# The gate table by one f32r matmul of 256 columns a token, split into a high and a low half

## What is computed

```python
qh = (xb @ w_query).reshape(tb, PEER_HEADS, 2, PEER_HALF)
scores = jnp.einsum('thpc,hpnc->thpn', qh, keys32)
val, idx = lax.top_k(scores, PEER_TOPK)
...
ids = jnp.take_along_axis(cand_id, pos, axis=-1).reshape(tb, PEER_HEADS * PEER_TOPK)
gate = jax.nn.softmax(top_s, axis=-1).reshape(tb, PEER_HEADS * PEER_TOPK)
```

## Time and profile before

| | |
|---|---|
| median of 3 runs | 3603.85 us (3603.44 to 3604.87) |
| the profiled execution | 3609.25 us, its span 3607.6 us |
| PE matmul busy | 3499.1 us, 97% |
| VectorE (DVE) busy | 1775.3 us, 49% |
| ScalarE (ACT) busy | 1278.5 us, 35% |
| GpSimd (POOL) busy | 509.7 us, 14% |

### The profile page before, as it was taken

The page is one execution under the profiler, slowest core; times in us unless marked ns, Lnnn a source line. Parts: engine busy times, 40 slices in busy tenths (PEclk is TensorE's granted clock), DMA queues, the critical chain, the costliest instruction groups (busy, mean ns, idle before and its releaser), DMA issues. The chain is left out here.

```text
span 3607.6 us, 52575 instructions
## 1 busy us (share of the span) xinstructions
PE 3499.1 (97%) x19436; PEld 2987.0 (83%) x19436; DVE 1775.3 (49%) x3405; ACT 1278.5 (35%) x1843; POOL 509.7 (14%) x434
## 2 busy tenths in 40 slices
PE   8998999999999999999999999998999999889999
PEld 8956787788888878888888799998889789768887
DVE  7344599566665224444444533335445456553333
ACT  4244222466665232222222332223223333333232
POOL 0100115433332001111111010010100000121011
PEclk9999999999999999999999999999999989989999
DMA  4200224355555546666666322222222100122232
GB/s 148 76 18 18 88 94 140 123 175 174 176 183 185 189 147 192 190 191 192 194 192 196 119 87 95 87 94 70 94 83 77 57 1 1 36 71 101 91 98 72
DMA packets 115447, 416.05 MB, mean 115 GB/s; under 512 B 14192, under 2 KB 14320, under 8 KB 113008
## 3 DMA queue, kind: packets, MB, share of 16 engines
q1 hardware_dynamic: 75632, 279.93, 23.6%
q0 software_dynamic: 18944, 67.12, 6.3%
q10 hardware_dynamic: 20736, 67.12, 4.9%
HBM read 344.91 MB, written 69.21 MB: 115 GB/s over the span
## 5 line engine op out<-in xcount | busy, mean ns | idle before, releaser
L444 DVE TENSOR_TENSOR w_lo<-ring,w_hi 128x1024 fp32r<-128x1024 f32 x224 | 275.5, 1230 | 695.6 <-ACT w_hi L440 695.5
L183 DVE TENSOR_TENSOR w_lo<-ring,w_hi 128x1024 fp32r<-128x1024 f32 (+2 forms) x157 | 205.9, 1312 | 571.5 <-ACT w_hi L177 571.5
L440 ACT ACTIVATE w_hi<-ring 128x1024 fp32r<-128x1024 f32 x255 | 270.1, 1059 | 504.4 <-PE ps L490 487.3
L460 PE MATMUL ps<-hn_hi,w_hi 128*128 128x512 f32 x1024 | 408.3, 399 | 3.0 <-POOL w_lo L444 1.4
L460 PE MATMUL ps<-hn_lo,w_hi 128*128 128x512 f32 x1024 | 404.8, 395 | 0.0
L460 PE MATMUL ps<-hn_hi,w_lo 128*128 128x512 f32 x1024 | 403.1, 394 | 0.0
L490 PE MATMUL ps<-units_hi,w_hi 128*128 128x512 f32 x1024 | 398.4, 389 | 2.7 <-DVE units_lo L801 2.7
L490 PE MATMUL ps<-units_hi,w_lo 128*128 128x512 f32 x1024 | 398.4, 389 | 0.0
L490 PE MATMUL ps<-units_lo,w_hi 128*128 128x512 f32 x1024 | 398.3, 389 | 0.0
L177 ACT ACTIVATE w_hi<-ring 128x1024 fp32r<-128x1024 f32 (+2 forms) x170 | 190.2, 1119 | 470.1 <-PE ps L241 379.7
L241 PE MATMUL ps<-f_hn_hi,w_hi 128*128 128x264 f32 (+1 forms) x1056 | 283.6, 323 | 19.8 <-DVE f_hn_lo L861 19.1
(11 more groups left out here) (434 smaller groups left out, 6719.2 us busy)
## 6 DMA issues: line engine op xcount, KB each, us to landing
ring<-in_w_uv SPq DMA_DIRECT2D x256, 512.0 KB, 3.4
ring<-in_f_up SPq DMA_DIRECT2D x88, 512.0 KB, 3.3
expert_units<-scratch ACTq DMA_DIRECT2D x128, 256.0 KB, 2.6
gate_table<-peer ACTq DMA_DIRECT2D x16, 2048.0 KB, 7.2
peer<-gate_table POOLq DMA_DIRECT2D x32, 1024.0 KB, 7.7
peer<-expert_units POOLq DMA_DIRECT2D x128, 256.0 KB, 3.7
ring<-in_w_in SPq DMA_DIRECT2D x29, 512.0 KB, 3.3
ring<-in_w_late SPq DMA_DIRECT2D x25, 512.0 KB, 3.3
```

The source lines that it names most:

```text
L183: self.nc.vector.tensor_tensor(self.l[:, self.slot(k), 0:self.cols], e.ring[:, self.ring(k), 0:self.cols], self.h[:, self.slot(k), 0:self. ...
L440: A_(uh[:, slot(n)], e.ring[:, ring(n), 0:D], ACT.Copy).then_inc(e.hi_done, 1)
L444: ops.tensor_tensor(ul[:, slot(n)], e.ring[:, ring(n), 0:D], uh[:, slot(n)].bitcast(F32), ALU.subtract).then_inc(e.lo_done, 1)
L460: mm = M(e.ps[:, n % 2, :], u[:, slot(n), ch * P:(ch + 1) * P], x[part][:, ch, META:L], start=(ch == 0 and j == 0), stop=(ch == DC - 1 and ...
```

## The change

A token's outer product becomes one f32r matmul: the stationary side is the column one-hot in f32r, the moving side 256 columns wide, with the row one-hot times the high part of the gate and the row one-hot times the low part side by side. The gate is split once for all tokens into `tb.gates` (high by ScalarE, low by VectorE). A batch now fills two PSUM banks, with two batches in turn instead of four. ScalarE copies the high half to an SBUF buffer (`high`), and VectorE adds the low half to it from PSUM and writes the table (`evac`, now VectorE's). VectorE makes no columns any more; ScalarE makes those of all odd batches. `hots` writes into 4 places in place of 8. VectorE's queue for each tile is now `hots`, `lo`, `hots`, `evac`, `evac`.

```diff
         def outers(it, m):
...
-            if r % 4 == 1:
-                pe.wait_ge(hot_act, it * 4 + (m // 4 + 1))
+            pe.wait_ge((hot_pool, hot_act)[m % 2], it * 8 + (m // 2 + 1))
             pe.wait_ge(stored, it * 16 + (m + 1))
             for t in range(GT):
-                mm = M(e.ps[:, 4 + m % 4, t * P:(t + 1) * P], tb.cols[:, r, t], tb.rows[:, r, t])
+                mm = M(both(m)[:, t].rearrange("p x i -> p (x i)"), tb.cols[:, m % GR, t],
+                       tb.rows[:, m % 4, t].rearrange("p x i -> p (x i)"))
...
-        def evac(it, m):
-
-            blk = m // BK
-            if m % BK == 0:
-                act.wait_ge(saved[blk], it * 16 + 16)
+        def high(it, m):
+
             act.wait_ge(outer, it * 16 + (m + GR + 1))
...
+            A_(tb.high[m % 2], both(m)[:, :, 0], ACT.Copy).then_inc(copied, 1)
...
-                A_(y[:, n * P:(n + 1) * P], e.ps[:, 4 + n, j * P:(j + 1) * P], ACT.Copy)
...
+            A_(tb.gates[:, n * P:(n + 1) * P, 0], e.ps[:, 4 + n, 2 * P:3 * P], ACT.Copy).then_inc(spread, 1)
...
-        columns(0, 1)
-        columns(0, 5)
+        for m in (1, 3, 5):
+            columns(0, m)
...
         def table_step(it, n, more):
             hi(act, it, 8, AHEAD + n + 1)
+            if more:
+                columns(it, 2 * n + 7)
             gelu(it, 8, AHEAD + n)
             spill(it, 8, AHEAD + n - 1)
-            evac(it, 2 * n)
-            evac(it, 2 * n + 1)
-            if n % 2 == 0 and more:
-                columns(it, 2 * n + 1 + GR)
+            high(it, 2 * n)
+            high(it, 2 * n + 1)
...
         def hots(it, m):
...
-            dve.wait_ge(outer, it * 16 + (m + 1))
+            dve.wait_ge(outer, it * 16 + (m + GR - 4 + 1))
...
-                oh = V.tensor_scalar(tb.rows[:, r, t], c["iota"], e.rowT[:, bass.ds(col, 1)],
-                                     e.gateT[:, bass.ds(col, 1)], ALU.is_equal, ALU.mult)
-                if r % 4 == 3:
-                    oh = V.tensor_scalar(tb.cols[:, r, t], c["iota"], e.colT[:, bass.ds(col, 1)], None,
-                                         ALU.is_equal)
+                oh = V.scalar_tensor_tensor(out=tb.rows[:, m % 4, t],
+                                            in0=c["iota"].unsqueeze(1).broadcast_to([P, 2, P]),
+                                            scalar=e.rowT[:, bass.ds(col, 1)],
+                                            in1=parts.unsqueeze(2).broadcast_to([P, 2, P]),
+                                            op0=ALU.is_equal, op1=ALU.mult)
...
+        def evac(it, m):
...
+            dve.wait_ge(copied, it * 16 + (m + 1))
+            t0 = (m % BK) * GT
+            V.tensor_tensor(tb.table[:, blk].rearrange("p i t -> p t i")[:, t0:t0 + GT, :], tb.high[m % 2],
+                            both(m)[:, :, 1], ALU.add).then_inc(stored, 1)
+
+        def table_step(it, n, more):
+            if more:
+                hots(it, 2 * n + 2)
+            lo(dve, V, it, 8, AHEAD + n + 1)
+            if more:
+                hots(it, 2 * n + 3)
+            evac(it, 2 * n)
+            evac(it, 2 * n + 1)
...
+        V.tensor_tensor(tb.gates[:, :, 1], e.gateT, tb.gates[:, :, 0].bitcast(F32), ALU.subtract).then_inc(parted, 1)
+        dve.wait_ge(parted, 1)
+        hots(0, 0)
+        hots(0, 1)
```

More of the change, by code:

```diff
@@ L418, in phase_peer @@
     hot, hot_pool, hot_act = e.sem("hot"), e.sem("hot_pool"), e.sem("hot_act")
+    parted, copied = e.sem("gate_parts"), e.sem("high_copied")
     pool_offset, act_offset = e.sem("pool_offset"), e.sem("act_offset")
@@ L445, in lo, with both @@
                           ALU.subtract).then_inc(e.lo_done, 1)
+    def both(m):
+        at = (4 + 2 * (m % 2)) * WIDE
+        return e.psf[:, at:at + 2 * WIDE].rearrange("p (t x i) -> p t x i", t=GT, x=2)
     def sp_program(sp):
@@ L482, in mix @@
                 if first and o == 4:
-                    pe.wait_ge(stored, batches + 4)
+                    pe.wait_ge(stored, batches + 2)
                 if first and o == 0:
@@ L528, in act_program @@
             act.sem_inc(saved[s], 16)
-        act.sem_inc(stored, 4)
         def gelu(it, step, n):
@@ L548, in columns @@
             off.then_inc(act_offset, 1)
-            act.wait_ge(act_offset, it * 4 + (m // 4 + 1))
-            A_(tb.cols[:, m % GR], tb.cols[:, m % GR], ACT.Relu, bias=e.one, scale=-1.0).then_inc(hot_act, 1)
-        def evac(it, m):
-            blk = m // BK
-            if m % BK == 0:
-                act.wait_ge(saved[blk], it * 16 + 16)
+            act.wait_ge(act_offset, it * 8 + (m // 2 + 1))
+            A_(tb.cols[:, m % GR], tb.cols[:, m % GR].bitcast(F32), ACT.Relu, bias=e.one,
+               scale=-1.0).then_inc(hot_act, 1)
+        def high(it, m):
             act.wait_ge(outer, it * 16 + (m + GR + 1))
-            t0 = (m % BK) * GT
-            A_(tb.table[:, blk].rearrange("p i t -> p t i")[:, t0:t0 + GT, :],
-               e.ps[:, 4 + m % 4, :].rearrange("p (t i) -> p t i", t=GT), ACT.Copy).then_inc(stored, 1)
+            A_(tb.high[m % 2], both(m)[:, :, 0], ACT.Copy).then_inc(copied, 1)
         def save(it, blk):
-            act.wait_ge(stored, it * 16 + (BK * (blk + 1) + 4))
+            act.wait_ge(stored, it * 16 + (BK * (blk + 1) + 2))
             act.dma_start(e.gtab[it * 2 + blk],
@@ L606, in act_program @@
         for n in range(8):
-            table_step(SPREAD // 8 - 1, n, n < 4)
+            table_step(SPREAD // 8 - 1, n, n < 5)
         with act.Fori(0, REST // 4) as it:
@@ L646, in equal @@
         def equal(j):
-            nc.gpsimd.tensor_scalar(tb.cols[:, 2 * j], tb.cols[:, 2 * j], 0.0, None,
+            nc.gpsimd.tensor_scalar(tb.cols[:, 2 * j], tb.cols[:, 2 * j].bitcast(F32), 0.0, None,
                                     ALU.is_equal).then_inc(hot_pool, 1)
@@ L778, in hots @@
-            oh.then_inc(hot, 1)
+                parts = tb.gates[:, bass.ds(col, 1)].bitcast(F32).rearrange("p o x -> p (o x)")
+                oh = V.scalar_tensor_tensor(out=tb.rows[:, m % 4, t],
[3 more added lines that the diff above has]
+                                            op0=ALU.is_equal, op1=ALU.mult)
@@ new lines, in hots @@
+            oh.then_inc(hot, 1)
+        def evac(it, m):
+            blk = m // BK
+            if m % BK == 0:
+                dve.wait_ge(saved[blk], it * 16 + 16)
+            dve.wait_ge(copied, it * 16 + (m + 1))
[10 more added lines that the diff above has]
+            evac(it, 2 * n + 1)
@@ L780, in dve_program @@
         dve.wait_ge(e.lo_done, base + AHEAD)
         lo(dve, V, 0, 8, AHEAD)
+        dve.sem_inc(stored, 2)
         dve.wait_ge(spread, nb)
-        with dve.Fori(0, SPREAD // 8) as it:
+        V.tensor_tensor(tb.gates[:, :, 1], e.gateT, tb.gates[:, :, 0].bitcast(F32), ALU.subtract).then_inc(parted, 1)
+        dve.wait_ge(parted, 1)
+        hots(0, 0)
+        hots(0, 1)
+        with dve.Fori(0, SPREAD // 8 - 1) as it:
             for n in range(8):
-                hots(it, 2 * n)
-                hots(it, 2 * n + 1)
-                lo(dve, V, it, 8, AHEAD + n + 1)
+                table_step(it, n, True)
@@ L788, in dve_program @@
+        for n in range(8):
+            table_step(SPREAD // 8 - 1, n, n < 7)
         with dve.Fori(0, REST // 4) as it:
@@ L2885, in hybrid_kernel @@
             a, tb = Arena(region), Env()
-            tb.rows, tb.cols = a.take(GR, GT, P), a.take(GR, GT, P)
+            a.take(2 * GR * GT * P)
+            tb.rows = work.at("hot_rows", 0, GR // 2, GT, 2, P, dt=F32R)
+            tb.cols = work.at("hot_cols", 4 * GR * GT * P, GR, GT, P, dt=F32R)
+            tb.gates = work.at("gate_parts", room + 12 * T, T, 2, dt=F32R)
+            tb.high = [x[:, 0:GT * P].rearrange("p (t i) -> p t i", t=GT) for x in (e.r0, e.r1)]
             tb.table = a.take(2, NK, GB)
```

7 lines of the change are left out of this document (1 added, 6 removed).

## The result

The changed kernel takes 3612.53 us (median of 8 runs, 3605.17 to 3623.41) against 3603.77 (8 runs, 3601.93 to 3607.81) of the kernel before: ratio 1.0023, interval 1.0013 to 1.0033. It is slower by 9 us, where 41 were forecast. The profiled execution took 3608.44 us (span 3606.8), so its rows belong to a run some 4 us under the median.

A forecast was written before the change was run, and what follows sets the result against it. VectorE was to become the bound: 6.54 us of own work, 1.04 lost to GpSimd's subtraction and 0.4 to its compare, 7.98 us a round against 7.34. Over 64 rounds +41, plus 2 at the start: 3645 us, range 3565 to 3715.

The forecast's parts named there:

- the side it gave 0.65: The changed kernel is slower than the one before: chance 0.65, against same 0.10 and faster 0.25.
- PE's round: TensorE per round: tile 5.63 us plus eight 256-column outer products 0.95 us, 6.58 us, down from 7.34.
- eight hots: VectorE's eight 128x256 one-hot row instructions per round: 0.40 us each, 3.2 us.
- low copy: VectorE's subtraction for the low weights, once a round, unchanged at 1.14 us.
- lost to the compare: GpSimd's compare gets in between two VectorE hots: 0.4 us a round, bounds 0 and 1.5.
- so I hold the write to be the limit, and take 1.1: VectorE's eviction pays for the table write stepping 32 words: 1.1 us each, two a round 2.2 us.
- the estimate of 1.15: Upper bound for one VectorE eviction, paying the stepped write in full: 0.61 + 0.54 us.
- the estimate of 0.95: Lower end of an eviction's 0.95 to 1.36 us by the skill's figures, noted as speaking against the change.
- Its 1.04 us is lost each round: GpSimd's subtraction falls in front of VectorE's hots every round and blocks them: 1.04 us, bounds 0 and 1.04.
- which covers the copy's 1.06: ScalarE's save wait delays its weight copy about 2 us; VectorE's four hots (1.6 us) first cover the 1.06 us copy.
- The costs meet near zero: Rival: evictions of 0.95 to 1.05 us and a free compare, rounds 7.28 to 7.48, 3602 to 3615 us; within 0.2%: 0.10.
- PE stays the bound: Rival: VectorE writes the stepped table at its dense rate, rounds of 6.58 us, 3557 us; chance 0.15.

The follow-up runs named there:

- e1: Changed kernel with VectorE's eviction writing the table densely, without the step, so the table is laid out wrongly: 3571.43 us, ratio 0.9913.
- e3: Changed kernel with GpSimd's compare left out and its subtraction kept: 3599.08 us, ratio 0.9981.
- e16: Changed kernel with ScalarE's and GpSimd's first loop turns written out and GpSimd's subtraction held until VectorE's last hots before the evictions: 3554.81 us, ratio 0.9866.
- e11: As e9, but with the very first save put back in its old place: 3556.6 us, 3553.84 to 3598.36, ratio 0.9881.
- e8: Changed kernel with two accumulating 128-column f32r matmuls per token, no high copy or addition, ScalarE evicting as before: 3607.73 us, ratio 1.0008.
- e12: As e9, but with saves issued behind ScalarE's column copies too: 3563.77 us, 3556.8 to 3602.63, ratio 0.9877.
- e9: Changed kernel with each save issued behind the next tile's weight copy and ScalarE's first turn written out: 3559.79 us, ratio 0.988.

## Why the prediction was right in direction, by luck, and wrong in size

It said 3645 us; 3612.5 was measured, in its range and on the side it gave 0.65. The step that failed is the price of VectorE's round: 7.98 us in every round was forecast, and 7.30 was measured in the slow pace and 6.51 in the fast one. Neither is above the 7.34 of before, so the mechanism forecast, as large as it really is, would have left the time where it was, or a little below. That it is slower comes from terms that the sum had at nothing or too small (turn starts, saves, the start of the stage). So the direction was luck. Terms of a round, forecast against measured (PE's in the fast pace, all others in the slow one, rows at 950.70 to 958.00):

| | forecast | measured |
|---|---|---|
| PE's round | 6.58 | 6.51 |
| eight hots | 3.2 | 3.14 (2 x 1.57) |
| low copy | 1.14 | 1.14 |
| two evictions | 2.2 | 1.87 |
| lost to the subtraction | 1.04 | 0.80 |
| lost to the compare | 0.4 | 0.35 |
| VectorE's round | 7.98 | 7.30 |
| saves and turn starts, over eight rounds | 0 | 61.3 - 8 x 7.31 = 2.8 |

- **PE, hots, low copy**: right within 0.07 us each. Eight outers take 0.95 us (1.11 as a group), as forecast from the earlier trace rows.
- **The evictions, the term most mis-sized.** The step "so I hold the write to be the limit, and take 1.1" was right in kind (e1: the stepped write costs 0.435 us) and wrong in size: one starts 0.94 us after the other. 1.1 is what one *lasts* (1113 ns); in the round only the distance from start to start counts, and the estimate of 1.15 was built by adding ScalarE's difference of *lengths* to VectorE's distance. 0.33 us a round, 21 us in all. The Trainium skill, "Vector Engine (DVE) Microarchitecture Reference", section 5.2, with 1.71 ns a column for 4 KiB hops would have given the estimate of 0.95 that the prediction noted and did not take; the trace agrees with that estimate (0.94 us), and not with the 1.36 from the page's 2.5 ns for a step of 24 words, though the step here, 32 words, is near the latter.
- **"Its 1.04 us is lost each round"**: true in one of two paces only. The sum made the stall follow from VectorE's own 6.54 us against PE's 6.58. With 6.15 VectorE has 0.36 us to spare, and the stall arises only once it has been made late; then 6.15 + 1.15 = 7.30 exceeds PE's round and the lateness feeds itself. The size of the stall was 0.24 too large: the held hot lasts 0.77 us longer beside a subtraction of 1.04; by 64 rounds that is 15 us. Why it is less than the whole 1.04 no run here shows.
- **The compare** was taken between the bounds at 0.4 and cost 0.35 (e3, 13 us). The Trainium skill, "SBUF — State Buffer", section "Who interferes with whom", by which the whole 1.5 us would be lost, is borne out in kind for the two-input subtraction (the hot that is 0.79 us late at 897.95) and not for this one-input compare.
- **ScalarE's wait in save, priced at nothing ("which covers the copy's 1.06")**, and the start of a turn, not priced: here the error went the other way. A turn of slow rounds costs 2.8 us over eight such rounds, with a wait of up to 5.3 us on ScalarE where 2 were given, and the table loads, which the trace of before had, were overlooked because they were hidden there.
- **The sum.** Slow rounds cost what they did before (7.30 to 7.34 us). In the profile, the 62 rounds from the second outer products to the last take 461.48 us, 455.08 before (711.08 to 1166.16). Of these, the five turns from 761.66 to 1064.68 take 303.0 where 40 rounds of 7.34 us are 293.6: +9.4; the other 22 rounds, many of the fast ones among them, give 3 back. The stage's start (second outer products at 714.75, not 711.08) costs 3.7, where 2 were forecast; PE's matmuls at the lower clock, which no term had, are 2.4 us of that stretch. That is +10 against a measured +9. The forecast's 64 x 0.64 = +41 is gone with the 0.68 us a round that the table shows.
- **Rivals.** "The costs meet near zero" (3602 to 3615, an eviction of 0.95 to 1.05 us) is where the time came out, though with the compare not free and the turn starts in its place. "PE stays the bound" (3557) is e16's case: it was one wait and a few loads away.

## What to carry to other kernels

When two engines with near-equal rounds share a resource, ask not only whether the round fits, but whether it fits again once one of them is late: if a late engine meets a stall that an early one passes by, the loop can have two paces, and a wide scatter of times can be their mark (3554 to 3598 us in e11, 3554 to 3555 in e16). Then tie the colliding instruction to the event that opens the safe gap (here one added wait, worth 42 us), before moving work about. A wait of TensorE can cost more than its own length, so look at the granted clock behind it. When an engine's slack goes, list what the old trace hid at loop turns, table loads and waits in an in-order queue among it; and where an experiment wins, look in its trace for what else its edit changed.

## What the runs showed of the hardware

- A write to SBUF with a step of 32 words at every element costs VectorE 1113 ns in place of 678 for 512 elements (0.94 us from start to start), and ScalarE 1135 in place of 595.
- f32r matmuls with a weight load each: 0.107 us at 128 columns (e8), 0.119 at 256. Below 256 columns there was next to nothing to gain.
- A two-input operation on GpSimd that came 1.16 us behind VectorE's first hot made the fourth 0.79 us late (e12); at 1.15 us it made none late and waited itself (e9).
- GpSimd's one-input compare of 1.5 to 1.7 us cost VectorE's two-input hots 0.35 us a round.
- Behind waits of 2.6 to 3.2 us TensorE's granted clock stood at 0.50 (1.2 GHz) for 3 to 5 us in three places of the changed kernel, with matmuls of 512 columns 0.43 us apart in place of 0.23; behind equal waits of 2.61 us at 945.87 and 1007.20 it stayed at 1.00.
